# A two-network forward pass on one core: feed-forward down by token rows in seven block products for eight

## What is computed

```python
    x = x + rmsnorm(m @ w_out[i], mix_post_norm[i])
    h = rmsnorm(x, ffn_pre_norm[i])
    f = (jax.nn.silu(h @ w_gate[i]) * (h @ w_up[i])) @ w_down[i]      # w_gate, w_up 1024x2816, w_down 2816x1024
    x = x + rmsnorm(f, ffn_post_norm[i])
    e = rmsnorm(p[i] @ w_ple_proj[i], ple_norm[i])
    x = x + jax.nn.sigmoid(x @ w_ple_gate[i]) * e                     # w_ple_gate 1024x1024
```

## Time and profile before

| | |
|---|---|
| median of 3 runs | 1956.88 us (1956.62 to 1957.73) |
| profiled execution, its own time | 1958.46 us |
| its span, first to last instruction | 1956.7 us |
| TensorE matmuls busy | 1938.3 us, 99% |
| VectorE busy | 1205.2 us, 62% |
| ScalarE busy | 880.1 us, 45% |
| GpSimd busy | 603.0 us, 31% |
| mean granted clock of TensorE | 0.999 |
| feed-forward and gate on TensorE | about 240 to 650 us |

### The profile page before, as it was taken

One profiled execution on the slowest core, in us unless ns is written; L12 is line 12 of the kernel. 1 busy time (PEld: TensorE's weight loads), 2 busy tenths in 40 slices (PEclk: granted clock), 3 DMA queues, 4 the chain that ended last, 5 costly groups with the idle time before them and its releaser, 6 DMA issues.

```text
span 1956.7 us, 23662 instructions
## 1 busy us (share of the span) xinstructions
PE 1938.3 (99%) x9216; PEld 1609.5 (82%) x9216; DVE 1205.2 (62%) x1701; ACT 880.1 (45%) x1284; POOL 603.0 (31%) x442
## 2 busy tenths in 40 slices
PE   8999999999999999999999999999999999999998
PEld 7877878888888888888888888888888888888886
DVE  7667763332257854545455857668566676866757
ACT  7445543332234552525245534444455555444435
POOL 2333645455455335353533000000333341000000
PEclk9999999999999999999999999999999999999999
DMA  5312367276322322222225557465322226746553
GB/s 164 94 44 76 97 98 116 93 123 112 94 86 87 119 76 94 79 87 85 86 86 151 128 173 179 123 172 129 107 86 85 86 65 183 173 128 172 122 179 86
DMA packets 166338, 221.31 MB, mean 113 GB/s; under 512 B 4640, under 2 KB 120096, under 8 KB 166112
## 3 DMA queue, kind: packets, MB, share of 16 engines
q1 hardware_dynamic: 151728, 190.52, 30.0%
q0 software_dynamic: 12928, 25.71, 7.7%
q10 hardware_dynamic: 1584, 3.74, 4.3%
...
## 4 chain that ended last, share of the span: by engine, by line
PE 89%; DVE 4%; ACT 2%; issue 2%; POOL 1%; DMA 1%; SPq 0%; DVEq 0%; ACTq 0%; POOLq 0%
PE ps L925 28%; PE ps L927 28%; PE ps L926 28%; PE ps L1097 1%; PE ps L1127 1%; POOL w_lo L819 1%; PE ps L1136 1%; PE ps L1137 1%; PE ps L1114 1%; DVE scr L2601 1%; DMA aux<-in_mlp_w 0%; PE ps L1467 0%; ACT w_hi L1612 0%; ACT w_hi L1630 0%; DVE w_lo L3011 0%
## 5 line engine op out<-in xcount | busy, mean ns | idle before, releaser
L819 POOL TENSOR_TENSOR w_lo<-raw,w_hi 128x512 fp32r<-128x512 f32 x376 | 529.8, 1440 | 667.4 <-ACT w_hi L1612 667.4
L925 PE MATMUL ps<-hn_hi,w_hi 128*128 128x512 f32 x1524 | 602.4, 395 | 2.2 <-DVE hn_lo L2710 1.7
L927 PE MATMUL ps<-hn_hi,w_lo 128*128 128x512 f32 x1524 | 593.8, 390 | 0.0
L926 PE MATMUL ps<-hn_lo,w_hi 128*128 128x512 f32 x1524 | 593.7, 390 | 0.0
L925 PEld LDWEIGHTS ps<-hn_hi,w_hi 128*128 128x128 f32 x1524 | 286.4, 188 | 66.3 <-issue 4.1
L927 PEld LDWEIGHTS ps<-hn_hi,w_lo 128*128 128x128 f32 x1524 | 286.2, 188 | 60.6
L926 PEld LDWEIGHTS ps<-hn_lo,w_hi 128*128 128x128 f32 x1524 | 286.5, 188 | 58.9 <-issue 1.7
L1612 ACT ACTIVATE w_hi<-raw 128x2048 fp32r<-128x2048 f32 (+1 forms) x98 | 186.0, 1898 | 286.9 <-PE ps L927 286.8
L1630 ACT ACTIVATE w_hi<-raw 128x1024 fp32r<-128x1024 f32 x112 | 116.1, 1056 | 205.2 <-PE ps L927 205.0
L925 PE MATMUL ps<-w_hi,hid_hi 128*128 128x512 f32 x456 | 177.7, 390 | 0.2
L926 PE MATMUL ps<-w_lo,hid_hi 128*128 128x512 f32 x456 | 177.4, 389 | 0.0
...
...
## 6 DMA issues: line engine op xcount, KB each, us to landing
raw<-in_mlp_w SPq DMA_DIRECT2D x56, 1024.0 KB, 5.4
raw<-in_ret_w_in SPq DMA_DIRECT2D x24, 1024.0 KB, 5.2
aux<-in_mlp_w POOLq DMA_DIRECT2D x16, 1024.0 KB, 8.9
raw<-in_att_w_in SPq DMA_DIRECT2D x12, 1024.0 KB, 5.5
raw<-in_w_gate SPq DMA_DIRECT2D x11, 1024.0 KB, 5.4
raw<-in_w_up SPq DMA_DIRECT2D x11, 1024.0 KB, 5.3
raw<-in_w_down SPq DMA_DIRECT2D x8, 1024.0 KB, 8.0
raw<-in_ret_w_out SPq DMA_DIRECT2D x8, 1024.0 KB, 5.0
```

Source lines behind the costliest of these rows:

```text
L819: ins = pool.tensor_tensor(w_lo[:, slot, at], raw[:, slot, at], w_hi[:, slot, at].bitcast(F32), ALU.subtract)
L925: pe.matmul(o, hi, rhs_hi, start=start, stop=False, skip_group_check=True)
L926: pe.matmul(o, hi, rhs_lo, start=False, stop=False, skip_group_check=True)
L927: return pe.matmul(o, lo, rhs_hi, start=False, stop=stop, skip_group_check=True)
```

## The change

**Groups 0 and 1 of down.** The 1024 hidden rows of a group and the 1024 output columns are cut in two halves each, the 512 tokens too (early and late). Of the eight products of a block of 512 rows, 512 columns and 256 tokens, seven are made, of sums and differences: of hidden parts (`t1` to `t4`, VectorE) and of weight blocks. The weight sums S3, S1 and S4 are made by GpSimd's transfers that add (`ffn_weight_sums`), M by VectorE. The stationary operand is now the hidden part (128 tokens), the moving one the weights (512 columns), so the result has tokens on the partitions; VectorE adds or subtracts it into `x_tok`, the same memory as `o_buf`. The order is A11, A12, S3, M, A21, S1, S4. Their low parts are made by VectorE, in halves of 1024 columns, no longer by GpSimd. The third group (6 tiles) is multiplied in full, also by token rows: left columns first, then right columns tile by tile.

**r.** Up is no longer multiplied by r; the product of SiLU and raw up frees the up banks. The r of a token comes in as a scale of rows: `ffn_r_columns` turns it into four columns.

**The norm.** ScalarE squares and sums rows (`ffn_square`), `ffn_row_scaled` scales them, TensorE turns them back (`turn_back`, 16 transposes for 256 tokens), VectorE adds them to `x` with the gain, and high and low parts of two feature tiles x 256 tokens follow.

**The gate.** Nothing is set apart. Chunks 0 and 1 are multiplied by halves of the tokens (`gate_half`): chunk 0 early, turn back of the late tokens, chunk 1 early, chunk 0 late, chunk 1 late.

The statistic of `e_buf` is taken behind group 0's fourth gate chunk; its sums lie between the up blocks.

```diff
-FFN = Phase(PROJ, [1] * 12, 2)
-FFN_LAST = Phase(FFN, [1] * 10)
-GATE = Phase(FFN_LAST, [1] * 4)
+FFN = Ffn(PROJ)
+GATE = Phase(FFN, [1] * 4)
...
-N_FPOST = Norm(N_PLE, 8, 0)
+N_FPOST = Norm(N_PLE, 0, 0, by_tokens=True)
...
+            def ffn_weight_sums(g):
+
+                w_down = T["w_down"][0, 0:2048, :].rearrange("(g a k p) (f c) -> g a f p k c", g=2, a=2, p=P, f=2)
+                s3 = s3_m_s4.rearrange("p (k c) -> p k c", k=4)
+                pool.wait_ge(s["s3_in"], FFN.landed(g))
+                pool.dma_start(s3, w_down[g, 1, 1], accum_op=ALU.add).then_inc(s["s3_added"], 16)
+                slot = FFN.raw_slot(g, FFN.load_s1(g))
+                s1 = raw[:, slot, :].rearrange("p (k c) -> p k c", k=4)
+                pool.wait_ge(raw_ready[slot], FFN.loads(g, FFN.load_s1(g)))
+                pool.dma_start(s1, w_down[g, 0, 1], accum_op=ALU.add).then_inc(s["s1_added"], 16)
+                pool.wait_ge(s["w_lo_ready"], FFN.ready(g, FFN.down(g, FFN.M), 1))
+                pool.dma_start(s3, w_down[g, 0, 0], accum_op=ALU.add).then_inc(s["s4_added"], 16)
+
+            for b in range(8):
+                ffn_up_lo(0, b, parts=b == 2)
+            ffn_weight_sums(0)
+            pool.wait_ge(s["w_lo_ready"], FFN.ready(1, 0, 1))
+            for b in range(1, 8):
+                ffn_up_lo(1, b)
+            ffn_weight_sums(1)
+            pool.wait_ge(s["w_lo_ready"], FFN.ready(2, 0, 1))
+            for b in range(1, 6):
+                ffn_up_lo(2, b)
+            pool.wait_ge(s["w_lo_ready"], GATE.chunk0)
+            for c in range(GATE.chunk0, GATE.chunk0 + 4):
+                lo(c, c % 2, parts=c < GATE.chunk0 + 3)
...
+                load_ffn_raw(g, 8, w_down[g, 0, 0], 4)
+                if g == 0:
+                    sp.wait_ge(s["norm_stat"], N_PLE.index + 1)
+                else:
+                    sp.wait_ge(s["w_lo_ready"], FFN.ready(0, FFN.down(0, FFN.S4), 1))
+                sp.dma_start(s3_m_s4.rearrange("p (k c) -> p k c", k=4), w_down[g, 1, 0]).then_inc(s["s3_in"], 16)
+                load_ffn_raw(g, 9, w_down[g, 1, 0], 4)
...
+            def ffn_r_columns():
+
+                pe.wait_ge(s["norm_r"], N_FFN.index + 1)
+                for t in range(4):
+                    ins = pe.matmul(ps[:, 6, t:t + 1], r_bc[:, t * P:(t + 1) * P], ident[:, 0:1], start=True, stop=True)
+                ins.then_inc(s["r_cols"], 1)
...
+            def ffn_product(g, n, what, bank, opens):
+
+                b, block = FFN.down(g, n), FFN_BLOCK[what]
+                hi, lo = (ap[:, FFN.slot(g, b), :].rearrange("p (k c) -> p k c", k=4) for ap in (w_hi, w_lo))
+
+                def step(k, t):
+
+                    at = slice(t * P, t * P + P)
+                    return three(ps[:, bank + t, :], hid_blocks[0][:, block, k, at], hid_blocks[1][:, block, k, at],
+                                 hi[:, k, :], lo[:, k, :], opens and k == 0, k == 3)
...
+            def ffn_down(g):
+
+                for n, what, bank, opens in ((FFN.A11, "b11", Z, g == 0), (FFN.A12, "b21", X, True), (FFN.S3, "t3", Y, True),
+                                             (FFN.M, "t2", X, False), (FFN.A21, "t4", Y, False), (FFN.S1, "t1", X, False),
...
+            def turn_back(half):
+
+                for q in range(4):
+                    if half == 0:
+                        pe.wait_ge(s["ffn_taken"], FFN.taken(2, FFN.LATE_LEFT))
+                        pe.wait_ge(s["fpost_row"], 2)
+                    else:
+                        pe.wait_ge(s["ple_x"], 2 * q + 2)
+                        pe.wait_ge(s["fpost_row"], 4)
+                    for f in (2 * q, 2 * q + 1):
+                        for n in range(2):
+                            ins = pe.transpose(turned_back(q)[:, f % 2, n * P:n * P + P],
+                                               x_tok[:, 2 * half + n, f * P:f * P + P], ident[:, :])
+                    ins.then_inc(s["fpost_t"], 1)
+
+            def ffn_end_right():
+
...
+                for t in range(2):
+                    for k in (4, 5, 0, 1, 2, 3):
+                        ins = ffn_end_step(k, 1, t)
+                    ins.then_inc(s["fpost_t"], 1)
+                for ks in ((4, 5), (0, 1), (2, 3)):
+                    for t in range(2, 4):
+                        for k in ks:
+                            ins = ffn_end_step(k, 1, t)
+                        if ks[0] == 2 and t == 2:
+                            ins.then_inc(s["fpost_t"], 1)
+                    ins.then_inc(s["group_done"], 1 + FFN.extra * (ks[0] == 2))
+                    if ks[0] == 0:
+                        turn_back(0)
...
+                    if (g, b) == (0, 6):
+                        for half in range(2):
+                            stat_halves(N_PLE, half, aux_halves)
+                        ffn_r_columns()
...
+            def gate_half(m, half):
+
+                c, g, tokens = GATE.chunk(m), GATE.group(m), (EARLY_TOKENS, LATE_TOKENS)[half]
+                hi, lo = (ap[:, c.slot, :].rearrange("p (k c) -> p k c", k=KD) for ap in (w_hi, w_lo))
+                wait = parts_ready(c, 11 + 3 * m)
+                if half == 0:
+                    group_empty(g)
+                    pe.wait_ge(s["ffn_taken"], FFN.taken(2, FFN.RIGHT + (1, 3)[m]))
+                for k in range(KD):
+                    if half == 0:
+                        wait(k)
+                    if k % 2 == 0:
+                        pe.wait_ge(s["ple_xlo"], 4 * half + k // 2 + 1)
                     for n in range(2):
...
+                        at = slice(n * P, n * P + P)
+                        ins = three(ps[:, g.bank(n), tokens], hi[:, k, at], lo[:, k, at], hn_hi[:, k, tokens],
+                                    hn_lo[:, k, tokens], half == 0 and k == 0, k == KD - 1)
+                if half:
+                    ins.then_inc(s["group_done"], 1)
...
-            c = GATE.chunk(0)
-            chunk_ready(c)
-            gate_product(0, range(GATE_SPLIT - 1), lambda k: pe.wait_ge(s["old_lo"], 2 * FFN_SPLIT + k + 1), stop=False)
-            stat(N_FPOST)
-            gate_product(0, range(GATE_SPLIT - 1, GATE_SPLIT), lambda k: pe.wait_ge(s["old_lo"], 2 * FFN_SPLIT + k + 1),
-                         start=False, stop=False).then_inc(s["gate_old_done"], 1)
-            for k in range(GATE_SPLIT):
-                pe.wait_ge(s["gate_e_lo"], k + 1)
-                for m in range(2):
-                    at = slice(m * P, m * P + P)
-                    ins = three(ps[:, 4 + m, :], hi[:, k, at], lo[:, k, at], gate_e_hi[:, k, :], gate_e_lo[:, k, :],
-                                k == 0, k == GATE_SPLIT - 1)
-            ins.then_inc(s["apart_done"], 1)
-            for m, k in ((0, 4), (1, 4), (0, 5), (1, 5), (0, 6), (0, 7), (1, 6), (1, 7)):
-                if (m, k) == (1, 4):
-                    chunk_ready(GATE.chunk(1))
-                gate_product(m, [k], gate_new, m == 1 and k == 4, m == 0 and k == 7)
-            gate_product(1, range(GATE_SPLIT), gate_new, start=False)
-            gate_product(2, range(KD), parts_ready(GATE.chunk(2), 12))
+            gate_half(0, 0)
+            turn_back(1)
+            gate_half(1, 0)
+            gate_half(0, 1)
+            gate_half(1, 1)
+            gate_product(2, range(KD), parts_ready(GATE.chunk(2), 17))
...
+            def ffn_square(t, f, taken):
+
+                act.wait_ge(s["ffn_taken"], FFN.taken(2, taken))
+                n = 2 * t + f
+                act.activation(scr[:, n + 1, :] if n < 4 else aux[:, n - 4, :], x_tok[:, t, 512 * f:512 * f + 512], ACT.Square, scale=ffn_r[:, t:t + 1],
+                               accum_out=mx[:, n:n + 1]).then_inc(s["fpost_sq"], 1)
+
+            def ffn_row_scaled(half):
+
+                two = slice(2 * half, 2 * half + 2)
+                act.wait_ge(s["fpost_sum"], half + 1)
+                act.activation(sm[:, two], sm[:, two], ACT.Ln, scale=1.0 / D, bias=eps[:, 0:1]).then_inc(s["fpost_r"], 1)
+                act.wait_ge(s["fpost_r"], 3 * half + 1)
+                for t in range(2 * half, 2 * half + 2):
+                    act.activation(r_col[:, t:t + 1], sm[:, t:t + 1], ACT.Exp, scale=-0.5, bias=ffn_log_r[:, t:t + 1])\
+                        .then_inc(s["fpost_r"], 1)
+                for t in range(2 * half, 2 * half + 2):
+                    act.wait_ge(s["fpost_r"], half + t + 2)
+                    act.activation(x_tok[:, t, :], x_tok[:, t, :], ACT.Copy, scale=r_col[:, t:t + 1])\
+                        .then_inc(s["fpost_row"], 1)
...
+                ffn_square(t, 1, FFN.RIGHT + t)
+            ffn_row_scaled(0)
+            split(GATE.chunk(0))
+            for q in range(2):
+                ffn_back_hi(0, q)
+            ffn_square(2, 1, FFN.RIGHT + 2)
+            ffn_back_hi(0, 2)
+            ffn_square(3, 1, FFN.RIGHT + 3)
+            ffn_back_hi(0, 3)
+            ffn_row_scaled(1)
+            split(GATE.chunk(1))
+            for q in range(4):
```

(22 more changed lines are left out.)

789 lines of the change are left out of this document (559 added, 230 removed).

## The result

| | before | changed |
|---|---|---|
| device time, median of 4 runs each | 1957.31 us | 1981.84 us (1980.70 to 1981.99) |
| ratio to before, 95% interval | | 1.0124 (1.0107 to 1.0142) |
| span of the profiled execution | 1956.7 us | 1978.8 us |
| mean granted clock of TensorE | 0.999 | 0.992 |

The change costs 24.5 us where 4.5 us of gain were forecast. The prediction missed in size and in sign. The first view to read is again the one on TensorE's waits over the whole span: waited for, us in total, times, longest.

The account below looks back on a forecast made before the run. TensorE, busy 99% of the span, was taken as the bound. Instructions -12.2, waits +1.0, +1.35 and +5.35 gave -4.5 us, taking the median from 1956.88 to 1952.4 us; range 1947.5 to 1958.

Parts of the forecast that it names:

- The two down phases: Down of groups 0 and 1: 38.1 us of TensorE each, VectorE's 34.8 us hidden, 0 wait; upper end 2 us a phase.
- Rival 2: Down phases do not hide their VectorE work: 2 us a phase, change -0.5 us, 1956.4 us; chance 0.20.
- TensorE's instructions: Matmuls and transposes over the changed stages: 17.5 us removed, 5.25 us added, net -12.2 us.
- the r columns: Four one-column matmuls that turn r into columns, 0.11 us each and a join: 0.5 us added.
- (a): Up block 3 of the first pair waits for the product with the SiLU to free banks: 1.0 us (0 to 1.3).
- (b): TensorE waits for the embedding norm's statistic behind pair 3's gate block: 1.35 us (0 to 1.7).
- The end: Norm by token rows and gate after group 2's down: waits of 5.35 us together, bounds 2.9 to about 10.
- Turn back 0: First transposing back of scaled rows, during group 2's down: no wait, 0.3 us to spare.
- Turn back 1: Transposing back of the late tokens' rows, between gate halves: waits 1.1 us for the scaled rows.
- half (1,0): Gate chunk 1, early tokens: waits 2.2 us for GpSimd's low-part quarters, ending at 53.05 us from group 2's down start.
- Half (0,0): Gate chunk 0, early tokens: waits 2.05 us for VectorE's low parts 1 and 2.
- rival 3: TensorE's clock falls to 1.2 GHz at the end, from turning back the late tokens: +12.8 us, 1969.7 us; chance 0.12.

Follow-up runs that it names:

- run 1: Changed kernel with the sixteen ext_rows transfers moved from behind the up pairs to the first and last retention head: 1954.72 us, ratio 0.9978.
- run 5: As run 1 and, besides, six instead of four of the eight squares and sums of the embedding statistic behind up pair 1: 1951.77 us, ratio 0.9968.
- run 7: Changed kernel, ext_rows transfers in their old places but reading a weight matrix row in DRAM instead of one SBUF partition: 1954.61 us, ratio 0.9985.
- run 9: Changed kernel, ext_rows transfers in their old places but reading 64 partitions of x in SBUF instead of one partition 64 times: 1954.16 us, ratio 0.9975.
- run 4: Changed kernel with only group 0's eight ext_rows transfers moved to the first retention head, group 1's eight left in place: 1964.67 us, ratio 1.0032.
- run 10: Changed kernel, rows of ext written to DRAM once, the sixteen spreads in their old places copying from there: 1955.21 us, ratio 0.9984.

## Why the prediction was wrong, step by step

**The step that failed** is "The two down phases", in the words "So I cost both phases at 0 wait". They waited 12.0 and 8.7 us, and the low clock behind these waits took 3.5 us more. What was wrong in it is the price of an adding transfer: 8.9 us, taken from the second network's MLP, where no `ext_rows` transfer runs. S3's took 21.75 us in group 0 and 30.02 in group 1. Its plain load took 12.9 us and landed 1.9 us before the phase (332.01, the phase starts at 333.94), where the prediction says "it lands some 5 us before the phase"; that alone would have cost nothing: with an add of 8.9 us S3's low part would have been there at about 343.6 us, and TensorE wanted it at 344.8. With the transfers out of the way (runs 1 and 5) the step nearly holds: 0.3 and 0.4 us of wait, both at M, which the prediction had 1.7 us ahead, and S3's add in group 0 took 12.7 us in run 5 and still landed some 2 us before it was needed. The bounds were of VectorE alone ("the upper end is 2 us a phase"). Rival 2 named S3's late sum and that "loads of 1024 KB lie beside it", but took its size from VectorE as well.

**TensorE's instructions** were right. SiLU of pair 1 of group 1 to SiLU of pair 0 of group 2, on ScalarE, in before and in run 5:

```profile
402.67 1.23 ACT L1990 ACTIVATE scr<-scr 128x512 f32<-128x512 f32 x2 [8.69 <-DVE scr L2414]
...
511.47 0.63 ACT L1990 ACTIVATE scr<-scr 128x512 f32<-128x512 f32 x1 [9.63 <-DVE scr L2414]
```

```profile
402.61 1.06 ACT L2391 ACTIVATE scr<-scr 128x1024 f32<-128x1024 f32 x1 [9.74 <-DVE scr L3326]
...
505.98 1.06 ACT L2391 ACTIVATE scr<-scr 128x1024 f32<-128x1024 f32 x1 [10.27 <-DVE scr L3326]
```

108.80 against 103.37 us: 5.43 us less, where 24 matmuls at 0.227 are 5.45. One small term was off. The predicted 0.5 us for the r columns, with the statistic itself:

```profile
316.25 0.39 PE L1134 MATMUL ps<-hn_hi,w_lo 128*128 128x512 f32 x1
316.72 0.51 PE L1175 MATMUL ps<-aux_halves,ones_r 128*128 128x512 f32 x1
317.44 0.51 PE L1175 MATMUL ps<-aux_halves,ones_r 128*128 128x512 f32 x1 [0.22 <-DVE aux_halves L2848]
317.79 0.95 PE L1504 MATMUL ps<-ident,scr 128*128 128x1 f32 x8
318.60 0.49 PE L1132 MATMUL ps<-hn_hi,w_hi 128*128 128x512 f32 x1
```

From 316.25 to 318.60 us are 2.35 us, 0.23 of it an ordinary start and 0.22 a wait; the statistic had cost 0.45 in the kernel before. That leaves 1.45 us, about 1.0 more than I put: the columns are eight instructions and take 0.81 us, and the statistic's two matmuls, which now start apart, take 0.64 us more than before.

**(a)** 1.3 us for 1.0, its upper bound. **(b)** 2.3 us for 1.35, above the upper end of 1.7; 1.9 us without the transfers (run 1). What (b) left out is the clock behind it: in run 1's profiled execution 78 matmuls were started from 320 to 340 us where 90 fit. With the columns just ahead the low clock cost 3.2 us by the starts, more than the wait.

**The end** waited 2.5 us for 5.35. Turn back 0 did not wait, as said. Turn back 1 waited 0.7 for 1.1 and half (1,0) 1.3 for 2.2, in the forecast order:

```profile
629.84 1.94 PE L1593 MATMUL ps<-ident,o_buf 128*128 128x128 f32 x16 [0.68 <-ACT o_buf L2482]
633.10 0.36 PE L1132 MATMUL ps<-hn_hi,w_hi 128*128 128x256 f32 x1 [1.32 <-POOL w_lo L995]
```

Half (0,0) waited 0.55 for 2.05. VectorE's low parts beside GpSimd took

```profile
619.99 0.98 DVE L3428 TENSOR_TENSOR hn_lo<-x,hn_hi 128x512 fp32r<-128x512 f32 x1
...
622.49 1.44 DVE L3428 TENSOR_TENSOR hn_lo<-x,hn_hi 128x512 fp32r<-128x512 f32 x1
...
625.23 1.47 DVE L3428 TENSOR_TENSOR hn_lo<-x,hn_hi 128x512 fp32r<-128x512 f32 x2
```

0.98, 1.44 and then about 0.75 each, where I had charged 1.65 for every one in the earlier trace rows: GpSimd was done at 625.07. **The clock at the end** (rival 3) stayed at 1.00: 32 transposes and 2.5 us of waits did not lower it. It fell behind the late statistic and at the two waits of the down phases, where the rival did not look.

So with the transfers gone the forecast is nearly met: -4.5 us forecast, -3.9 the median of run 1. That is in part luck, because its terms are off in both directions. For the profiled execution they add up so: -4.5, end -2.85, (a) and (b) +0.85, M +0.3, columns and statistic +1.0, clock +3.2, waits elsewhere +0.6 (the first weights of the kernel alone 1.3 more), together -1.4; its span is 1.9 us under before's. The last 0.5 us, here as in the changed kernel, are not placed. Not settled is what decides whether the clock falls: the waits of 1.9 us for the statistic stand in the profiled executions of five runs, and from 320 to 340 us the granted clock was 0.84 in run 1, 0.91 in run 7 and 0.86 in run 9, but 1.00 in runs 4 and 10.

**Why one partition is slow, and why the others suffer.** Where q10 is alone it moves 26 GB/s, and two transfers in flight take 12.5 us. The Trainium skill (SBUF — State Buffer, Door 1: The DMA port swizzle) states that a transfer's bandwidth depends on how many of 16 ports its partitions reach, and gives 27.6 GB/s for partitions 0 to 3, which share one. By that an estimate is 6 us for 160 KB and 12 for two in flight: the trace agrees. Runs 7 and 9 take the one partition away and keep the rest. No run reads several partitions that share a port, so these runs do not tell whether it is the one partition or its one port that is slow. Queues q1 and q0 slow down beside q10 in the rows above, though three different engines issue them; the Trainium skill (DMA: Bandwidth & Descriptors, Issuing engines are not separate DMA queues) states that all of them interleave on the same 16 DMA engines. Run 1 agrees: with q10 gone from the stage S3's load takes 5.1 us for 12.9. How an engine shares its time between a slow read and a fast one was not measured.
